# A decoder layer's attention inputs on one core: the stage behind the projection in a new order

## The reference

```python
mod = jax.nn.silu(c) @ ada_w + ada_b                  # six vectors of 1024 per sequence
h = rmsnorm(x, g1) * (1 + sc1) + sh1
nq, nkv, ng, mqkv, mif, mo, pu = split_cols(h @ w_in) # three head groups
o_nsa = compressed + selected blocks + window attention, mixed by sigmoid gates
hm, mstate = mlstm(mq, mk * HEAD_DIM ** -0.5, mv, ig, lf, mstate)
o_p, pool_state = pool_mix(pu, pool_prev, pos0, pool_w, pool_scale)
x = x + gt1 * (concat(o_nsa, sigmoid(mo) * hm, o_p) @ w_out)
h2 = rmsnorm(x, g2) * (1 + sc2) + sh2
f, ffn_state = conv_ffn(h2, ffn_prev, w_up, conv_w, conv_b, w_down)
x = x + gt2 * f
```

## Time and profile before

| | us |
|---|---|
| median of 3 runs | 853.15 (849.0 to 860.11) |
| profiled execution, its own time | 853.69 |
| its span | 851.9 |
| TensorE busy | 782.7 (92%) |
| mean granted TensorE clock | 0.952 of full speed |
| stage behind the projection | 217.5 to 281 |
| attention units | 281 to 385 |

### The profile page before, as it was taken

How to read it: one execution, slowest core, us unless ns; L and a number is a source line. 1 busy time by engine, 2 the same in 40 slices (tenths; PEclk the granted TensorE clock), 3 DMA queues, 4 the chain that set the end, 5 groups by cost and what they waited for, 6 DMA issues and landing times.

```text
span 851.9 us, 18750 instructions
## 1 busy us (share of the span) xinstructions
PE 782.7 (92%) x7517; PEld 720.7 (85%) x7517; DVE 504.3 (59%) x978; ACT 328.9 (39%) x601; POOL 297.3 (35%) x147
## 2 busy tenths in 40 slices
PE   2899989998998798998988999999999999999994
PEld 2788879987867565668988999999999999999993
DVE  3736877882494798763666666665212666665324
ACT  4432322323341266653335455443113455454221
POOL 0043555543000144451432344343443444343440
PEclk9999999998796699998999999999999999999997
DMA  9964867884559734504730344333223333322212
GB/s 355 337 207 155 249 225 252 270 257 158 207 190 377 157 103 125 129 6 170 293 99 28 121 103 125 112 102 109 86 89 112 106 118 112 99 78 98 86 59 100
DMA packets 73140, 131.22 MB, mean 154 GB/s; under 512 B 12684, under 2 KB 47388, under 8 KB 72800
## 3 DMA queue, kind: packets, MB, share of 16 engines
q1 hardware_dynamic: 66928, 114.32, 42.4%
q10 hardware_dynamic: 6096, 15.73, 5.4%
q0 software_dynamic: 32, 0.00, 0.0%
HBM read 124.56 MB, written 9.12 MB: 157 GB/s over the span
## 4 chain that ended last, share of the span: by engine, by line
PE 71%; DVE 14%; DMA 5%; SPq 3%; issue 3%; ACT 2%; POOL 2%; ACTq 0%; DVEq 0%; POOLq 0%
PE ps L665 53%; DMA arena<-cache_keys 3%; PE ps L1012 2%; PE ps L997 2%; PE ps L1034 2%; SPq L475 2%; PE ps L1050 2%; POOL arena L611 1%; DVE arena L1497 1%; PE ps L915 1%; DMA arena<-weights 1%; DMA raw<-weights 1%; DVE arena L2074 1%; DVE arena L1498 1%; DVE arena L1494 1%
## 5 line engine op out<-in xcount | busy, mean ns | idle before, releaser
L665 PE MATMUL ps<-hR,wR 128*128 128x260 f32 x3456 | 430.1, 286 | 15.6 <-POOL wR L631 7.7
L665 PEld LDWEIGHTS ps<-hR,wR 128*128 128x128 f32 x3456 | 423.4, 191 | 20.3 <-issue 14.6
L631 POOL TENSOR_TENSOR wR<-raw,wR 128x1024 fp32r<-128x1024 f32 x92 | 221.7, 2410 | 292.8 <-ACT wR L1132 292.8
L1132 ACT ACTIVATE wR<-raw 128x1024 fp32r<-128x1024 f32 x94 | 99.4, 1058 | 216.3 <-PE ps L665 210.0
L665 PE MATMUL ps<-fR,wR 128*128 128x260 f32 x1056 | 128.1, 283 | 2.3 <-DVE fR L2045 2.0
L665 PEld LDWEIGHTS ps<-fR,wR 128*128 128x128 f32 x1056 | 127.1, 188 | 3.1 <-DVE fR L2045 2.4
L2069 DVE COPY arena<-arena 128x2 f32<-128x2 f32 x44 | 47.7, 1084 | 93.6 <-ACT arena L1423 93.6
L623 POOL TENSOR_SCALAR arena<-arena,fac 128x128 f32<-128x128 f32 (+3 forms) x32 | 40.4, 1264 | 139.9 <-DVE fac L1968 139.9
L611 POOL TENSOR_TENSOR arena<-arena,par 128x1024 f32<-128x1024 f32 x16 | 34.7, 2170 | 99.3 <-DMA arena<-cache_keys 96.4
L2030 DVE TENSOR_TENSOR t<-ps,mod 128x8 f32<-128x8 f32 x24 | 4.0, 167 | 108.6 <-PE ps L665 108.6
L1356 ACT ACTIVATE arena<-ps,nmx 128x128 f32<-128x128 f32 (+3 forms) x64 | 33.1, 524 | 19.3 <-DVE nmx L1959 19.3
(11 more groups left out here) (369 smaller groups left out, 832.1 us busy)
## 6 DMA issues: line engine op xcount, KB each, us to landing
raw<-weights SPq DMA_DIRECT2D x95, 512.0 KB, 3.5
arena<-cache_keys SPq DMA_DIRECT2D x128, 192.0 KB, 3.5
arena<-weights SPq DMA_DIRECT2D x27, 512.0 KB, 10.3
arena<-cache_values SPq DMA_DIRECT2D x128, 64.0 KB, 2.0
raw<-weights ACTq DMA_DIRECT2D x12, 512.0 KB, 8.6
arena<-weights ACTq DMA_DIRECT2D x9, 512.0 KB, 8.4
x<-xT SPq DMA_DIRECT2D x16, 260.0 KB, 4.1
out_y<-x SPq DMA_DIRECT2D x8, 260.0 KB, 2.2
```

What stands on the lines that cost most here:

```text
L631: nc.gpsimd.tensor_tensor(w_slot(i)[:, 1, :, :], raw[:, g % RAW, :, :], w_slot(i)[:, 0, :, :].bitcast(F32), ALU.subtract).then_inc(lo_read ...
L665: last = mm(ps[:, a + half, 0:TH], w_slot(i)[:, wp, k, :], src[:, hp, j, half * TH:(half + 1) * TH], start=(j == 0 and q == 0), stop=(j == ...
L1132: A(w_slot(i)[:, 0, :, :], raw[:, g % RAW, :, :], ACT.Identity).then_inc(hi_ready, 1)
```

## The change

It reorders the stage's lists on all four engines and SyncE's behind it.

- SyncE copies the gate rows to DRAM ahead of the window keys. It issues the slots of all triples and of the output projection itself, then the two large outputs and the values of sample 0. Window 0, values 1, window 1, the state of the samples and the other outputs come behind `mmix_ready`.
- TensorE's triples stand apart from one another and earlier; the gate columns move to another bank and come last in `sample_rows`, where Q, K and V rows are now one product of 192 columns for each head; the pooled products go to banks 4 and 5 and come before triple 7; the head transposes come last, in banks 0 and 1. The first scores wait for `mmix_ready` in place of `side_mix`.
- ScalarE issues no weights. Its steps stand in the new order.
- VectorE's block maximum comes first; the selection is cut in three (`samples_compare`, `samples_ranks`, `samples_selection`); the prompt's compressed scores are cut in two; pooled result, gates and sample weights come ahead of heads 2 and 3.

Core of the diff (a line of "..." where lines are left out):

```diff
 
+            sp.wait_ge(rows_ready, 1)
+            sp.dma_start(spread, mro[0:4, :]).then_inc(side_landed, 16)
             sp.wait_ge(comp_done, 2 * NB)
             sp.wait_ge(slc_scored, 2 * NB)
             for b in range(0, NB, 4):
                 sp.dma_start(kwin[:, b:b + 4, :], winK[:, b:b + 4, :]).then_inc(win_landed, 16)
             sp.wait_ge(pooled_ready, NB)
             sp.dma_start(ltri[0:64, :], ltri_d).then_inc(ltri_landed, 16)
-            sp.wait_ge(rows_ready, 1)
-            sp.dma_start(spread, mro[0:4, :]).then_inc(side_landed, 16)
             sp.wait_ge(side_landed, 32)
             sp.wait_ge(slot_done, N_A)
-            for hh in range(2):
-                sp.dma_start(bc[hh], spread[hh:hh + 1, :].broadcast_to([P, S]).rearrange("p (i n) -> p i n", i=ST)).then_inc(bc_landed[0], 16)
+
+            def load_rows(hh):
+                sp.dma_start(bc[hh], spread[hh:hh + 1, :].broadcast_to([P, S]).rearrange("p (i n) -> p i n", i=ST)).then_inc(bc_landed[hh // 2], 16)
+
+            load_rows(0)
+            load_rows(1)
             for g in range(N_A + RAW, N_A + RAW + EXTRA):
                 load_slot(g)
-            for hh in range(2, 4):
-                sp.dma_start(bc[hh], spread[hh:hh + 1, :].broadcast_to([P, S]).rearrange("p (i n) -> p i n", i=ST)).then_inc(bc_landed[1], 16)
+            load_rows(2)
+            load_rows(3)
+            for g in range(N_A + RAW + EXTRA, len(PART1) + RAW):
+                load_slot(g)
+
             def load_values(b):
 
                 for half in range(2):
@@ -526,25 +533,24 @@
             def load_window(b):
                 sp.dma_start(vwin[:, b % 2], winV[:, b]).then_inc(vwin_landed[b % 2], 16)
 
+            sp.dma_start(o_fm, pT[:, T_KC:T_MK, 0:S]).then_inc(early_out, 16)
+            sp.dma_start(o_vn, vn[:, :, :]).then_inc(early_out, 16)
             sp.wait_ge(wsc_done, 2)
             load_values(0)
+            sp.wait_ge(slot_done, len(PART1))
+            sp.wait_ge(mmix_ready, 1)
+            load_window(0)
+            sp.dma_start(cst[:, :], mC).then_inc(rec_landed, 16)
             load_values(1)
-            sp.dma_start(cst[:, :], mC).then_inc(rec_landed, 16)
-
-            sp.dma_start(o_fm, pT[:, T_KC:T_MK, 0:S]).then_inc(early_out, 16)
-            sp.dma_start(o_vn, vn[:, :, :]).then_inc(early_out, 16)
+            load_window(1)
             sp.dma_start(o_st, sT[:, :, :]).then_inc(early_out, 16)
             sp.dma_start(o_snv, sn[0:NB, 7 * P:9 * P]).then_inc(early_out, 16)
             sp.dma_start(o_pool, pT[:, T_PU:T_PU + 2, S - 15:S]).then_inc(early_out, 16)
             sp.wait_ge(pool_ready, 1)
             sp.dma_start(o_spool, zs[:, :, :, 1:16]).then_inc(state_out, 16)
-            sp.wait_ge(mmix_ready, 1)
             for a in range(2):
                 sp.dma_start(o_C[:, a::2, :], stS[hr[a], :, ST - 1, :]).then_inc(state_out, 16)
             sp.dma_start(o_m, mout[0:4, 0:1]).then_inc(state_out, 16)
-            sp.wait_ge(slot_done, len(PART1))
-            load_window(0)
-            load_window(1)
 
             sp.wait_ge(early_out, 16 * 5)
             load_values(2)
@@ -804,38 +810,32 @@
             for j in range(4):
                 last = mm(ps[strips[j], 6, P:2 * P], con_("ones", 0, 32, 1), par_("bv", hi=1), start=False, stop=True)
             last.then_inc(blocks_done, 1)
...
+                    three = sn[0:NB, 0:768].rearrange("p (t h d) -> p t h d", t=3, h=4)[:, :, hh, :]
+                    mm(ps[:, 6, 0:192].rearrange("p (t d) -> p t d", t=3), sel, three, start=(hh == 0), stop=(hh == 3))
...
+                pe.wait_ge(g_exp, 1)
+                for h in range(NH):
...
-                    pe.wait_ge(g_exp, 1)
+                    pe.wait_ge(sg_exp, 1)
...
+            block_sums()
             triple(0)
+            sample_rows()
+            chunk_scores(0)
             compressed_scores()
-            gate_columns()
-            chunk_scores(0)
-            sample_rows()
-            block_sums()
             chunk_scores(1)
+            triple(1)
             triple_turn(0)
+            inside(0)
+            triple(2)
+            chunk_scores(2)
+            inside(1)
             window_scores(0)
-            triple(1)
-            inside(0)
+            triple_turn(1)
+            triple(3)
+            chunk_scores(3)
             window_scores(1)
-            chunk_scores(2)
-            triple_turn(1)
-            window_rows()
-            inside(1)
-            triple(2)
-            chunk_scores(3)
-            triple_turn(2)
-            triple(3)
             across(0)
             across(1)
+            triple(4)
+            triple_turn(2)
+            window_rows()
+            triple(5)
             triple_turn(3)
-            triple(4)
             inside(2)
+            triple(6)
             triple_turn(4)
             inside(3)
-            triple(5)
+            pooled_mix()
+            triple(7)
             across(2)
             across(3)
             triple_turn(5)
-            triple(6)
...
             triple_turn(6)
...
-            triple(7)
             triple_turn(7)
+            head_turns()
...
-                    pe.wait_ge(side_mix, 1)
+                    pe.wait_ge(mmix_ready, 1)
...
+            act.wait_ge(sx_in, 1)
+            A(scm[:, 0:NCB], scm[:, 0:NCB], ACT.Exp, bias=ssx[:, 1:2], scale=SCALE, accum_out=ssx[:, 2:3]).then_inc(sx_out, 1)
...
-            def load_weights(g):
-                act.dma_start(raw_slot(g), wst[g, :, :].rearrange("p (k n) -> p k n", k=KD)).then_inc(landed(g), 16)
...
-                for n in range(N_A + 3 * g, N_A + 3 * g + 3):
-                    if n in BEFORE:
-                        load_weights(BEFORE.index(n))
-
...
+            weights(0)
             triple_read(0)
-            weights(0)
+            weights(1)
...
             factors(0)
-            window_read(0)
             triple_read(1)
             weights(2)
-            window_read(1)
+            triple_read(2)
...
+            window_read(0)
+            triple_read(3)
+            act.wait_ge(pcx_ready, 2)
             A(pc[:, :, 0:NCP], pc[:, :, 0:NCP], ACT.Exp).then_inc(pcx_exp, 1)
-            triple_read(3)
+            window_read(1)
             act.wait_ge(sx_in, 2)
             A(sall[:, :], sall[:, :], ACT.Exp, bias=ssx[:, 7:8], scale=SCALE, accum_out=ssx[:, 8:9]).then_inc(sx_out, 1)
             triple_read(4)
...
+            def samples_block_max():
+
+                for moved in sst_moved:
+                    dve.wait_ge(moved, 64 * NB // 2)
+                V.tensor_reduce(bmax[:, 0:32], sall[:, 0:NPG * P].rearrange("p (n k) -> p n k", k=64), AX, ALU.max)
+
+            samples_block_max()
...
+
+            def samples_ranks():
+
...
+
+            def samples_selection():
+
...
+            samples_cmp_weights()
             masked_rows(0)
             masked_rows(1)
             exponents(0)
-            samples_cmp_weights()
+            samples_block_sums()
+            samples_compare()
+            samples_new()
+            weighted(0)
             prompt_cmp_scores()
-            weighted(0)
-            samples_new()
-            samples_block_sums()
+            samples_ranks()
             weighted(1)
             masked_rows(2)
             masked_rows(3)
             exponents(1)
-            samples_block_max()
+            prompt_cmp_max()
+            weighted(2)
+            states(0)
             samples_selection()
-            states(0)
-            weighted(2)
-            samples_window_max()
             weighted(3)
             head_result(0)
             head_result(1)
-            states(1)
+            samples_window_max()
             samples_output_gates()
             link(V.tensor_scalar(scm[:, :], scm[:, :], sg[:, 0:1], None, ALU.mult))
...
+            prompt_gates()
+            samples_weights(0)
+            prompt_cmp_weights()
+            states(1)
+            pooled_result()
             head_result(2)
             head_result(3)
-
...
+            samples_weights(1).then_inc(sp_ready, 1)
 
             dve.wait_ge(hT_done, 1)
-            windows_moved(dve)
-            V.tensor_tensor(mix[:, 4:6, 0:S], ps[:, 4:6, :], pT[:, T_MO:T_MO + 2, 0:S], ALU.mult).then_inc(mmix_ready, 1)
...
+            V.tensor_tensor(mix[:, 4:6, 0:S], ps[:, 0:2, :], pT[:, T_MO:T_MO + 2, 0:S], ALU.mult).then_inc(mmix_ready, 1)
```

More of the change, by code:

```diff
@@ L806, in _ @@
             last.then_inc(blocks_done, 1)
-            def gate_columns():
-                pe.wait_ge(sn_evac, 1)
-                pe.wait_ge(blocks_evac, NB + 1)
-                pe.wait_ge(pooled_ready, NB + 2)
-                for h in range(NH):
-                    last = mm(ps[0:64, 6, 400:403], pick[:, 7 - h:71 - h], sn[0:NB, 6 * P + 64 + 3 * h:6 * P + 67 + 3 * h],
-                              start=(h == 0), stop=(h == NH - 1))
-                last.then_inc(gates_done, 1)
             def block_sums():
```

125 lines of the change are left out of this document (63 added, 62 removed).

## The result

The changed kernel takes 868.04 us in the median of four runs, the kernel before 852.22 us; the ratio is 1.0168, 95% interval 1.0126 to 1.021. A second series of both gave 867.23 against 851.85 us, 1.0175 (1.0126 to 1.0224). It is **slower by 1.7%**, about 15 us, and lies above the range that was forecast (842 to 860). The profiled execution took 866.1 us.

The account below looks back on a forecast made before the run. The prediction took TensorE (busy 782.7 of 851.9 us) to bound the kernel, so only its idle time, clock or work pays. 853.7 - 8.0 (stage) + 6.1 (SyncE's queue) = 851.8 us, its own range 845 to 857, with rivals 842 to 860.

Parts of the forecast that it names:

- The rows out first: Stage front: gate rows about 4 us earlier; VectorE gains about 4, maximum first costs 0 to 1; TensorE alone unmoved.
- The stage's sum, 55.5 us: First triple to first score product: 45.0 work + 6.5 clock + 1.0 + 1.7 + 1.3 waits, against 63.4; 8 us gained.
- At half once, not twice: Sign to look for: TensorE's clock in the stage falls to half one time, costing 6.5 us.
- Waits at the end: Stage's end: TensorE waits 1.7 us for the last two heads, then 1.3 us for `mmix` with its latency.
- Weights: Weights on SyncE's queue land in 4.4 us; only triples 5 and 6 wait, 1.0 us in all.
- SyncE's queue: Behind the stage: window 2 issued at t0 (`mmix_ready`) + 42.2; TensorE waits 9.0 us, 2.9 comes back, cost 6.1.
- rival of a further fall: After the 9 us hole TensorE runs a stretch at 1.2 GHz, 6.0 us more: 857.8 us, chance 0.18.
- The sum: Whole kernel: 853.7 less 8.0 for the stage plus 6.1 for SyncE's queue, 851.8 us.
- "queue" rival: Outputs take their upper bound, window 2 lands at t0 + 50.2, cost 11.6 us: 857.3 us, chance 0.20.
- "clock" rival: Clock falls once more, behind the 9 us hole or in the stage, 6.0 us: 857.8 us, chance 0.18.

Follow-up runs that it names:

- e4: Kernel before, with only the block maximum moved first, ahead of the key memset: 854.78 us, ratio 1.0022 to the kernel before.
- e9: Changed kernel, with overwritten filler products on TensorE in the two gaps ahead of triple 0: 863.41 us, ratio 1.0106 to the kernel before.
- e1: Changed kernel, with the block maximum put back behind weighted(0): 854.88 us, ratio 1.0011 to the kernel before.
- e3: Changed kernel, with block maximum behind weighted(0) and window 2 loaded ahead of the value pages of sequences 2 and 3: 853.65 us, ratio 0.9995.
- e5: Changed kernel, with block maximum behind weighted(0) and every window load in SyncE's loop one sequence of pages earlier: 845.21 us, ratio 0.9936.
- e8: Changed kernel run again as it is, for a second time and trace: 867.23 us, ratio 1.0175 to the kernel before.
- e10: Changed kernel, maximum still first, with SyncE waiting for the last score moves before issuing the window keys: 857.15 us, ratio 1.0022.
- e11: e5 with weights of triples 2 to 7 and the output projection's first three issued by ScalarE, as before: 852.21 us, ratio 0.9976.
- e6: e5 with the compressed scores straight behind triple 0 and the sample rows behind them: 844.69 us, ratio 0.9923 to the kernel before.
- e7: e6 with triple 1 moved up, behind compressed scores and chunk scores 0 and ahead of the sample rows: 846.08 us, ratio 0.994.
- e12: Kernel before, with only SyncE's queue behind the weights in the new order: 857.38 us, ratio 1.0049.
- e2: Changed kernel, with window 2 loaded ahead of the value pages of sequences 2 and 3: 863.42 us, ratio 1.0094 to the kernel before.

## Why the prediction was wrong, step by step

- **The step that failed** is "The rows out first", and in it the price of the block maximum: "cost 0 to 1 us", "on TensorE alone it moves nothing". The step named its own condition, that the moves land late, and gave it neither a price nor a rival, though no row of the trace before showed the moves' landing. The moves land 5.4 us behind the projection's end in the changed kernel (4.6 in e4, 6.3 in e9). The cost is 5.2 us of late start and, through the clock, more: putting the maximum back is worth 12.4 us (14.0 by the ratios). I had also overlooked that `block_sums`, now ahead of triple 0, hangs on the same chain. The rows themselves were out early: e1's VectorE has them 6.2 us behind the projection's end, 3.6 earlier than before, where 4 was forecast. In the changed kernel VectorE came to them only at 220.97, and they gave nothing.
- **The stage's sum, 55.5 us.** Its mechanism holds once the maximum is out of the way: 54.0 us in e3 and e5 (58.4 in e1, with the longer stretch). In the changed kernel the terms are work 43.3 where I had 45.0, clock 16.6 for 6.5, and waits 3.35 for 4.0: 63.2. The clock is the term that failed. TensorE was busy at half clock for 31.1 us of the first stretch inside the stage and 2.0 of the last; 33.1 in all, half of it 16.6. The work of the kernel before was 44.8 and not 45.4, as its two stretches are 13.6 us long and my windows took 13.0 of each. "At half once, not twice" was right for the fall behind the weights in this trace, but not in e8, e10 or e11, and I did not see the fall at the stage's end. The length was not mine to take from the kernel before, where no gap came ahead.
- **Waits at the end**, 1.7 for the heads and 1.3 for `mmix`: 1.40 and 1.32. Right.
- **Weights.** One wait of 0.63 us where 1.0 was forecast; landing 6.0 us in the median and not 4.4. By the Trainium skill (Trainium Kernel Development and Optimization, Key Constraints) another issuing engine saves only the issue time. As far as the landing goes the rows agree: medians for the two sets of slots over the stage are 6.0 and 6.2 us on ScalarE's queue (e11), 6.7 and 6.1 on SyncE's in e5, 5.7 and 6.3 in the changed kernel. What the engine changes is when the load is issued, 1.7 us, and whether the values stand ahead of it. That I went by one row of 4.4 was wrong in its reason; the gain was larger than the 1.8 us I set against it, 3.4 to 7, for in e11's trace a wait of 1.78 us brings a second fall of the clock.
- **SyncE's queue.** Window 2 issued 40.0 us behind the first score product (42.2 forecast; the outputs took 4.3, near their lower bound, and not 7.7), landing in 3.1 us (2.5), wanted at 34.3 (35.7), hole 8.78 (9.0). The place and the size were right. The term was 7.5 us and not 6.1, and my reason for what comes back was wrong. Behind the hole nothing came back: third to fourth group is 14.21 us, 14.09 before. TensorE's idle time there did shrink, from 2.9 to 1.7 us, but its busy time grew from 11.2 to 12.5, as the clock was at half from 321.3 to 331.4. The 1.3 us that the hole is longer than the term came ahead of it, where the third group was ready 1.4 us sooner behind the first score product. So the rival of a further fall came true, at 1.7 us (half of 3.4 busy) and not 6.0.
- **The sum.** 853.7 - 8.0 + 6.1 should have read 853.7 + 5.2 - 0.2 + 7.5; with 1.0 of the rest and less the 1.0 of an earlier projection it gives 866.2, near the 866.1 of the profiled execution. The "queue" rival did not come, though the kernel is slower: its mechanism was outputs at their upper bound and a landing at t0 + 50.2, and it was 4.3 us and t0 + 43.1. The "clock" rival came in part, none held the maximum, and the range ended 8 us too low.

## What to carry to other kernels

A step moved into an idle time is free only if its own inputs are there: look for the landing of what it waits for, and if no row shows it, give the lateness a price and a chance of its own, for everything behind it in program order is late too. On a kernel that TensorE bounds, count a gap twice, once as waiting and once as the half-speed stretch that can follow. When a late load is moved ahead in a queue, write out when each later load is issued and wanted; moving one moved the hole, moving all of them by one place took it away and, with the maximum back in its place, made the reordered kernel 0.6% faster than the one before (0.8% with e6).

## What the runs showed of the chip

- The last of four moves of 16 KB between partitions landed about 9 us after its issue beside 2 MB of loads on another queue, and about 2 us after it without them (e10).
- The granted clock fell to half at most 2.3 us behind the end of waits for weights of 1.25 us (e10), 1.67 (e8), 1.70 (e7), 1.78 (e11), 1.85 (e12) and 2.17 us (e6), and in the kernel before behind 0.60 and 1.13 us close together. It did not fall behind single waits of 0.62, 0.63 and 1.13 us (e3, changed kernel, e2).
- With gaps of 2.6 to 2.8 and 1.2 to 1.4 us ahead of triple 0 it stayed at 1.2 GHz for 34.0 us in the three traces there are (changed kernel, e8, e2), though TensorE was busy 32.81 of them; for 27.2 us in e4, with one gap of 1.8 us and the old order; and for 6.8 to 20.5 us in the new order without the late start.
